# Unused one-pass matmuls at stage borders of the second block of a two-block layer kernel

## The chip, the cores and the metric

The kernel runs on one core of a Trainium2 chip. The metric is the device time of one execution in microseconds (us); the median of three runs is given. TensorE is called PE here, VectorE DVE, ScalarE ACT, GpSimd POOL, and SyncE, which issues most transfers, SP.

## What is computed

Two transformer-like blocks run one after the other on 512 tokens of width 1024. The first one is a convolution branch and a windowed attention, followed by a layer of 16384 experts of which each token picks 16 in each of 8 heads. The second one, where nearly all of the change lies, is cut to its shape here:

```python
def second_block(x, mem, positions, norm_g, ..., w_out):
    h = rms_norm(x, norm_g[l])
    p = h @ w_in[l]
    (p_r, p_k, p_v, p_w, p_a, z_a, p_q, p_sk, p_sv, z_b,
     p_xq, z_c, p_gate) = jnp.split(p, split_points, axis=-1)
    y_a = rwkv7_mix(p_r, p_k, p_v, p_w, p_a, ...) * silu(z_a)
    y_b = sliding_window_sink_attn(p_q, p_sk, p_sv, positions, ...) * silu(z_b)
    y_c = memory_cross_attn(p_xq, mem, ...) * silu(z_c)
    gates = sigmoid(p_gate).reshape(bsz, t, 3, D_MODEL)
    merged = (gates[:, :, 0] * (y_a @ w_proj_a[l]) + gates[:, :, 1] * (y_b @ w_proj_b[l])
              + gates[:, :, 2] * (y_c @ w_proj_c[l]))
    return x + merged @ w_out[l]
```

## The kernel before

The program is a row of stages. Each stage is a block in which every engine has its own hand-written order of instructions, and at the end of a block all five engines wait for one another. No instruction of the next block starts on any engine before the slowest one has arrived; in the order of PE this shows as a branch that waits for the release of a barrier. Below, a border is such a place, and the release is the moment at which all engines go on.

Large products run in units of 24 matmuls. A unit is one 128 wide column block of weights, 8 pieces deep. Both operands are held as a high and a low part in a rounded 32-bit format (fp32r), and `product` (lines 152 to 156) makes three one-pass matmuls of 128 x 512 of each piece: high by high, low by high, high by low. The weights of a unit come through a ring. SP loads them (L197), ACT makes the high part (L205) and POOL the low part (L222). `hT` is the normalised input, transposed, as high and low part, and it stays in place for the whole block.

The second block has 46 units that no stage needs at once: gates and projections used later. They are the work of the class `Filler`. Each stage calls `fill.pe(pe, steps)`, and a step is one piece, so three matmuls. Their results go through banks 6 and 7, are copied by ACT (L293) and stored to DRAM by SP (L302). What is left at the end is done by `catch_up`, which waits for the stores. The stages of the second block that the change touches, in order:

- `project_tiles` (rwz): 13 units with `hT`, whose weights are there when the stage begins.
- `rwkv_prepare`: four fp32 matmuls L2001 that wait for a tanh of ACT, filler steps, four more (L2007), filler steps.
- `rwkv_solve`, which runs four times, t from 0 to 3: 16 small fp32 matmuls of 64 rows (L2171, 32 records in the profile), then filler steps.
- `fetch`, run three times (rwgate, swz, xqz): SP brings a part of the stored results back, ACT applies Silu (L1786), PE does 3, 14 or 8 filler steps.
- `rotate`: DVE turns queries and keys (L1901 to L1903) while PE does 18 filler steps.
- `attention` (attn2) follows it: for each of 32 pairs of a token block and a head, scores (L497), softmax on DVE and ACT, a transposing product (L507), the values (L519), and one filler step.
- `rms_over_partitions` (xqnorm): ACT squares four tiles, PE sums them (L1672), DVE and ACT make the root, PE does two filler steps, spreads the root (L1681) and does eight more.
- `catch_up`: the last filler unit.
- `merge_second`: 12 units with the three branches' outputs. PE waits for DVE's high and low parts (L2608, L2610), and DVE multiplies by gates and adds (L2620, L2626).
- `out_residual` (wout2): 8 units into eight banks, then DVE adds x (L1029) and SP stores the output.

Of the kernel before, what the change touches and what calls it, by code (L numbers as in the profile page):

```python
# [27 lines left out]
P = 128  # L28
# [208 lines left out]
        return Split(self.high[:, u % 2], self.low[:, u % RING])  # L237


class Filler:  # L240


# [66 lines left out]
            sp.wait_ge(self.stored[i], 16 * ((self.sent + 1 - i) // 2))  # L309


def catch_up(nc, fill):

    with nc.Block() as block:
        @block.tensor
        def _(pe):
            fill.pe(pe, DT * FILL2)

        @block.scalar
        def _(act):  # L320
            fill.act(act, fill.done)

        @block.sync
        def _(sp):
            fill.sp(sp)
            fill.wait_stored(sp)

        @block.gpsimd
        def _(pool):
            fill.w.low_parts(pool)  # L330
# [341 lines left out]
def first_block(nc, w, bank, cols, const, rows, subkeys, given, x, hT, mem_store, dump):  # L672

    ident, ones = const.whole("ident"), const.whole("ones")
    with ExitStack() as outer:
        attnT = split_tensor(nc, outer, "attnT", [P, DT, T])

        z_store = nc.dram_tensor("z1_store", (FILL1, P, T), F32, kind="Internal").ap()
        with ExitStack() as inner:
            conv = split_tensor(nc, inner, "convT", [P, DT, T])  # L680
            convT = conv.whole
            qkvT = inner.enter_context(nc.sbuf_tensor("qkvT", [P, 12, T], F32))
            norm_to_T(nc, w, bank, "norm1", x, TT, cols.whole("norm1"), ident, hT, first_unit("z1") + RING)
# [14 lines left out]
            units = []  # L698
            for b in range(TT):
                lo, hi = max(b - 1, 0), min(b + 2, TT)  # L700
                for i in range(8):
                    for e in range(2):
                        h = HEADS1[i][e]
                        a, part = i // 4, slice(e * HD, (e + 1) * HD)
                        kv = 2 * a + e
                        units.append(dict(
                            q=qkvT[part, i, b * P:(b + 1) * P], k=qkvT[part, 8 + a, lo * P:hi * P],
                            bias=(const.whole("dist")[:, (lo - b + 1) * P:(hi - b + 1) * P], -SLOPES[h] * HD ** 0.5),
                            v=[v_tok[:, c, kv * HD:(kv + 1) * HD] for c in range(lo, hi)],
                            sink=cols("sink", h), sink_scaled=sink8[:, h:h + 1], half=e))  # L710
            at = lambda g: (slice(None), slice(4 * (g % 2), 4 * (g % 2) + 4), slice((g // 2) * P, (g // 2 + 1) * P))
            attention(nc, bank, "attn1", units, scale=HD ** -0.5, sink=True, ident=ident,
                      out=lambda g: attnT.high[at(g)], out_low=lambda g: attnT.low[at(g)], group=8, dim=HD, fill=fill,
                      fill_steps=2)
            catch_up(nc, fill)
            assert fill.done == FILL1
        with ExitStack() as inner:
            mergedT = split_tensor(nc, inner, "mergedT", [P, DT, T])
            merge_first(nc, w, bank, z_store, attnT, mergedT)
            out_residual(nc, w, bank, "wout1", mergedT, x, first_unit("query") + RING, 0.5)  # L720
    dump("x1", x)
    with ExitStack() as inner:
        h2 = inner.enter_context(nc.sbuf_tensor("h2", [P, TT, D], F32))
        score_store = nc.dram_tensor("score_store", (TT, PH, P, 2, NKEYS), F32, kind="Internal").ap()
        norm_to_T(nc, w, bank, "norm2", x, TT, None, ident, hT, first_unit("query") + RING, scaled=h2,
                  row_gain=rows[:])
        experts(nc, w, bank, cols, const, ident, subkeys, score_store, h2, hT, given["peer_uv"], x, rows[:],
                given["rows1"][:, D:2 * D], given["mem"], mem_store)
    dump("y", x)
# [250 lines left out]
                    split_merged(nc, dve, mergedT, f, high_ready)  # L980


def out_residual(nc, w, bank, name, mergedT, x, prefetch, scale, store=None):


    with Stage(nc, name) as st:
        ready, added, stored = st.sem("ready"), st.sem("added"), st.sem("stored")
        u0 = first_unit(name)
        with st.block() as block:
# [8 lines left out]

            @block.tensor
            def _(pe):  # L1000
                for k in range(DT):
                    ring = w.wait(pe, u0 + k)
                    for t in range(TT):
                        for e in range(2):
                            mm = product(nc, bank[2 * t + e][:], mergedT[:, k, t * P:(t + 1) * P],
                                         ring[:, 4 * e:4 * e + 4], k == 0, k == DT - 1)
                            if k == DT - 1 and (t, e) != (TT - 1, 1):
                                mm.then_inc(ready, 1)
                    mm.then_inc(w.done, 1)
# [614 lines left out]
def project_tiles(nc, w, bank, name, unit, count, src, takers, prefetch, loads=()):  # L1624
# [3 lines left out]
    with Stage(nc, name) as st:  # L1628
        kept, loaded = st.sem("kept"), st.sem("loaded")
        u0 = first_unit(unit)  # L1630
        with st.block() as block:
# [9 lines left out]
            def _(pe):  # L1641
                def four_tiles(i, first, count=RING):
                    for j in range(count):
                        ring = w.wait(pe, u0 + j, i)
                        if not first:

                            pe.wait_ge(kept, i * RING + (j - RING + 1))
                        for k in range(DT):
                            mm = product(nc, bank[j][:, 0:width], ring[:, k], src[:, k], k == 0, k == DT - 1)
                        mm.then_inc(w.done, 1)  # L1650
                rounds(pe, count // RING, four_tiles)
                if count % RING:
                    four_tiles(count // RING, False, count % RING)
# [32 lines left out]
def rms_over_partitions(nc, bank, name, tiles, gains, selector, ident, fill, steps):  # L1686
# [5 lines left out]
    with Stage(nc, name) as st:  # L1692
# [4 lines left out]
        with st.block() as block:  # L1697
            @block.tensor
            def _(pe):
                for i in range(len(tiles)):  # L1700
                    pe.wait_ge(squared, i + 1)
                    mm = group_sums(nc, bank[0][:, i * columns:(i + 1) * columns], sq[:, i], selector)
# [39 lines left out]
def second_block(nc, ctx, w, bank, a, x, hT, mem_store, out, dump, load):  # L1742
# [18 lines left out]
    y_low = [same_place(nc, f"y{n}T_low", y_shape, o) for n, o in zip("abc", offsets)]  # L1761
    sliding_branch(nc, w, bank, a, cols, const, yT[1], dump, load, fill)
    memory_branch(nc, bank, cols, const, mem_store, yT[2], dump, fill)
    catch_up(nc, fill)
    with ExitStack() as s:
        mergedT = split_tensor(nc, s, "merged2T", [P, DT, T])
        merge_second(nc, w, bank, yT, y_low, z_store, mergedT)
        out_residual(nc, w, bank, "wout2", mergedT, x, sum(n for _, n in UNITS), 1.0, store=out)


def fetch(nc, name, fill, first, z, silu, steps, more=()):

    n = z.shape[1]
    with Stage(nc, name) as st, st.block() as block:
        arrived, done = st.sem("arrived"), st.sem("done")

        @block.tensor
        def _(pe):
            fill.pe(pe, steps)

        @block.scalar
# [21 lines left out]
def memory_branch(nc, bank, cols, const, mem_store, y, dump, fill):  # L1803

    ident, ones = const.whole("ident"), const.whole("ones")
    with ExitStack() as s:
        kv = s.enter_context(nc.sbuf_tensor("mem_kv", [P, 2, 1024], F32))
        kT, v_tok = (kv[:, e].rearrange("p (a b) -> p a b", a=n) for e, n in ((0, 4), (1, 2)))
        qz = s.enter_context(nc.sbuf_tensor("xqz", [P, 8, T], F32))
        fetch(nc, "xqz", fill, 14, qz[:], 4, 8, [(kv[:], mem_store)])  # L1810
        rms_over_partitions(nc, bank, "xqnorm", [qz[:, n] for n in range(4)], 4 * [cols.whole("xq_g")], ones[:, 0:1],
                            ident, fill, (2, 8))
        units = [dict(q=qz[:, h, b * P:(b + 1) * P], k=kT[:, h], bias=None,
# [14 lines left out]
def sliding_branch(nc, w, bank, a, cols, const, y, dump, load, fill):  # L1828

    ident = const.whole("ident")  # L1830
    with ExitStack() as s:
# [1 line left out]
        z = s.enter_context(nc.sbuf_tensor("swz", [P, 10, T], F32))  # L1833
        v_tok = s.enter_context(nc.sbuf_tensor("vs_tok", [P, TT, P], F32))
        sink8 = s.enter_context(nc.sbuf_tensor("sink8_2", [P, 8], F32))
        fetch(nc, "swz", fill, 4, z[:], 6, 14)
        rms_over_partitions(nc, bank, "sqknorm", [z[:, n] for n in range(5)], 4 * [cols.whole("q_g")] + [cols.whole("k_g")],
                            const.whole("halves")[:, 0:P:HD], ident, fill, (3, 10))
        turn_tiles(nc, w, bank, "turn_vs", [([z[:, 5, t * P:(t + 1) * P]], v_tok[:, t]) for t in range(TT)], ident, 0)
# [21 lines left out]
def rotate(nc, bank, a, cols, const, z, load, fill):  # L1861
# [7 lines left out]
    with Stage(nc, "rope") as st:  # L1869
# [8 lines left out]
        with st.block() as block:  # L1878
# [27 lines left out]
            def _(pe):  # L1906
                for i in range(5):
                    nc.tensor.matmul(bank[i][:], const.whole("swap"), z[:, i], start=True, stop=True).then_inc(swapped, 1)
                fill.pe(pe, 18)

            @block.scalar
            def _(act):
# [15 lines left out]
def rwkv_branch(nc, w, bank, a, cols, const, hT, y, dump, load, fill, tables):  # L1928
# [7 lines left out]
    with ExitStack() as s:  # L1936
# [24 lines left out]
            rwkv_output(nc, bank, const, t, R, B, Kt, toks, ZW, WT, S, y, fill)  # L1961

        gate = toks["A"]
        fetch(nc, "rwgate", fill, 0, gate[:], 0, 3)
        rwkv_finish(nc, bank, cols, halves, ident, y, bonus, gate, toks["B"], dump, fill)


def rwkv_prepare(nc, bank, a, cols, const, z, R, A, B, Kt, bonus, r_end, toks, load, fill):
    halves = const.whole("halves")
    with Stage(nc, "rwprep") as st:  # L1970
# [6 lines left out]
        with st.block() as block:  # L1977
# [18 lines left out]

            @block.tensor
            def _(pe):
                pe.wait_ge(tanh_ready, 1)
                for t in range(TT):  # L2000
                    nc.tensor.matmul(bank[t][:], tl[0:CH, t * P:(t + 1) * P], lora[0:CH, :], start=True,  # L2001
# [150 lines left out]
def rwkv_solve(nc, bank, const, t, A, B, Kt, toks, ZW, WT, y, fill):  # L2152
# [4 lines left out]
    with Stage(nc, f"solve{t}") as st:  # L2157
# [6 lines left out]
        with st.block() as block:  # L2164
            @block.tensor
            def _(pe):

                for e, left in enumerate((B, Kt)):
                    for h in range(8):
                        part, c, cols = head(h)  # L2170
# [371 lines left out]
    dump("ya", y)  # L2542


def merge_second(nc, w, bank, yT, y_low, z_store, mergedT):


    u0, g0 = first_unit("merge"), FILL2 - 24
# [5 lines left out]
    with Stage(nc, "merge2") as st:  # L2554
# [7 lines left out]
        with st.block() as block:  # L2562
# [11 lines left out]
            @block.tensor  # L2574
            def _(pe):

                for n in range(12):
                    ring = w.wait(pe, u0 + n)
                    if n >= 2:
# [207 lines left out]
```

## Time and profile before

| | us |
|---|---|
| median of three runs | 2996.11 |
| lowest and highest run | 2995.95, 2999.30 |
| profiled execution, its own time | 2995.75 |
| span of the trace, first to last instruction | 2993.9 |
| PE busy | 2505.0 (84%) |
| DVE busy | 1741.2 (58%) |
| mean granted PE clock | 0.954 |

The profile lists the work of each engine by kernel line, with what released an engine from a wait. "PEq" as releaser is PE's own sequencer: at a stage's first matmul that is the border. The granted clock of PE is 1.00 at 2.4 GHz and 0.50 at 1.2 GHz. The busy length of one matmul record has the pipeline's depth in it, so the pace of a row of matmuls is read as a stretch of time divided by the matmuls in it. The second block runs from 2032 us to the end.

### The profile page before, as it was taken

The numbers are of one execution on the slowest core, as the hardware profiler recorded it, in microseconds if no ns is written. First come the engines' busy times: TensorE is split into PE (matmuls) and PEld (weight loads), VectorE is DVE, ScalarE is ACT, GpSimd is POOL, SyncE is SP. The second block draws the span as 40 slices with busy tenths as digits, with TensorE's granted clock in tenths as the row PEclk, the third lists the DMA queues.
The fourth block names the chain that finished last, engine by engine and source line by source line (L and its number), as shares of the span: only waits on it lengthen the run. The fifth ranks groups of instructions, "written<-read, shape, count | busy, mean of one in ns | idle before, by whom it ended". The sixth has DMA issues, their size and how long they took to land. (4 is left out here: it accounts for less than half of the span.)

```text
span 2993.9 us, 30870 instructions
## 1 busy us (share of the span) xinstructions
PE 2505.0 (84%) x10382; PEld 1601.2 (53%) x10382; DVE 1741.2 (58%) x3956; ACT 892.5 (30%) x1997; POOL 848.8 (28%) x649
## 2 busy tenths in 40 slices
PE   6997999978987788777777777778889999789888
PEld 4885666765543343222222232227678887555766
DVE  5998556536776777667766676650353332255353
ACT  3223434133333243223322232222322220234331
POOL 0001110435544455334333343323221110111133
PEclk9998999989999998999999999999899999879899
DMA  3332111429999999999999999972121110221242
GB/s 119 109 104 76 61 46 50 137 96 404 422 421 420 421 419 418 421 421 416 417 413 416 413 411 422 406 328 92 63 65 53 43 54 23 92 67 42 85 156 91
DMA packets 132922, 683.46 MB, mean 228 GB/s; under 512 B 13472, under 2 KB 24992, under 8 KB 66976
## 3 DMA queue, kind: packets, MB, share of 16 engines
q0 software_dynamic: 73728, 536.90, 43.3%
q1 hardware_dynamic: 59040, 144.61, 14.5%
q8 instruction: 83, 1.36, 0.2%
q14 instruction: 71, 0.58, 0.1%
HBM read 655.77 MB, written 25.69 MB: 228 GB/s over the span
## 5 line engine op out<-in xcount | busy, mean ns | idle before, releaser
L1611 PE MATMUL bank<-peer_uv,peer_diag 128*128 128x512 f32 x2048 | 965.7, 616 | 295.0 <-ACT peer_diag L1284 294.7
L1511 DVE SCALAR_TENSOR_TENSOR peer_uv<-peer_uv,h 128x1024 f32<-128x1024 f32 x512 | 642.2, 1265 | 383.0 <-DMA peer_uv<-in_peer_uv,peer_index 382.9
L1611 PEld LDWEIGHTS bank<-peer_uv,peer_diag 128*128 128x128 f32 x2048 | 382.8, 195 | 838.0 <-issue 833.5
L1319 POOL DMA_INDIRECT peer_uv<-in_peer_uv,peer_index x512 | 529.8, 1035 | 747.4 <-PE bank L1611 662.2
L222 POOL TENSOR_TENSOR weight_low<-weight_ring,weight_high 128x1024 fp32r<-128x1024 f32 x107 | 260.5, 2435 | 1308.4 <-ACT weight_high L205 1308.4
L154 PE MATMUL bank<-hT_high,weight_high 128*128 128x512 f32 x952 | 416.6, 438 | 34.3 <-POOL weight_low L222 13.4
L155 PE MATMUL bank<-hT_low,weight_high 128*128 128x512 f32 x952 | 382.6, 402 | 0.0
L156 PE MATMUL bank<-hT_high,weight_low 128*128 128x512 f32 x952 | 381.9, 401 | 0.0
L205 ACT ACTIVATE weight_high<-weight_ring 128x1024 fp32r<-128x1024 f32 x171 | 180.6, 1056 | 578.5 <-PE bank L156 490.6
L1279 ACT ACTIVATE peer_gelu<-peer_dots 128x2 f32<-128x2 f32 x256 | 52.0, 203 | 789.4 <-DVE peer_uv L1511 789.3
L154 PEld LDWEIGHTS bank<-hT_high,weight_high 128*128 128x128 f32 x952 | 186.0, 195 | 93.3 <-issue 38.3
L1284 ACT ACTIVATE peer_diag<-const,peer_weight 128x128 f32<-128x128 f32 x512 | 177.5, 393 | 118.7 <-DVE peer_weight L1423 117.8
L155 PEld LDWEIGHTS bank<-hT_low,weight_high 128*128 128x128 f32 x952 | 186.3, 196 | 41.4 <-issue 9.6
L156 PEld LDWEIGHTS bank<-hT_high,weight_low 128*128 128x128 f32 x952 | 185.6, 195 | 41.6
L548 DVE SCALAR_TENSOR_TENSOR attn_logit<-const,bank 128x256 f32<-128x256 f32 (+2 forms) x96 | 43.5, 453 | 122.2 <-PE bank L497 122.2
L507 PE MATMUL bank<-attn_diag,attn_prob 128*128 128x128 f32 x496 | 83.7, 295 | 9.1 <-issue 5.4
L507 PEld LDWEIGHTS bank<-attn_diag,attn_prob 128*128 128x128 f32 x496 | 65.3, 191 | 48.2 <-issue 36.5
L827 DVE SCALAR_TENSOR_TENSOR convT_whole<-z_u,cols,convT_whole 128x512 f32<-128x512 f32 x120 | 89.5, 746 | 0.0
L827 DVE SCALAR_TENSOR_TENSOR z_odd<-z_u,cols,z_odd 128x512 f32<-128x512 f32 x112 | 83.6, 746 | 0.0
L1423 DVE SCALAR_TENSOR_TENSOR peer_weight<-peer_gelu,peer_r,peer_e 128x2 f32<-128x2 f32 x256 | 59.0, 230 | 38.9 <-ACT peer_gelu L1279 38.9
L611 ACT ACTIVATE attn_sinkexp<-cols,attn_negtop 128x1 f32<-128x1 f32 x96 | 28.3, 294 | 156.5 <-DVE attn_negtop L557 156.4
L230 POOL TENSOR_TENSOR weight_low<-weight_ring,weight_high 128x1024 fp32r<-128x1024 f32 x24 | 58.0, 2415 | 46.8 <-ACT weight_high L205 46.5
(393 smaller groups left out, 3243.7 us busy)
## 6 DMA issues: line engine op xcount, KB each, us to landing
weight_ring<-in_weights SPq DMA_DIRECT2D x171, 512.0 KB, 3.6
z_store<-fill_stage SPq DMA_DIRECT2D x70, 256.0 KB, 2.7
peer_uv<-in_peer_uv,peer_index POOLq DMA_INDIRECT x512, 14.1
merge_z<-z_store SPq DMA_DIRECT2D x8, 768.0 KB, 4.9
merge_z<-z_store SPq DMA_DIRECT2D x12, 512.0 KB, 4.6
score_store<-peer_work SPq DMA_DIRECT2D x16, 256.0 KB, 13.9
peer_sc<-score_store SPq DMA_DIRECT2D x24, 128.0 KB, 8.7
swz<-z_store SPq DMA_DIRECT2D x1, 2560.0 KB, 9.9
```

The source lines that it names most:

```text
L154: nc.tensor.matmul(to, left[0], right[0], start=start, stop=False)
L155: nc.tensor.matmul(to, left[0], right[1], start=False, stop=False)
L156: return nc.tensor.matmul(to, left[1], right[0], start=False, stop=stop)
L205: self.nc.scalar.activation(self.high[:, u % 2].bitcast(F32R), self.ring[:, u % RING], ACT.Copy).then_inc(self.high_ready, 1)
L222: self.nc.gpsimd.tensor_tensor(self.low[:, slot].bitcast(F32R), self.ring[:, slot], self.high[:, u % 2], ALU.subtract).then_inc(self.split, 1)
L507: mm = nc.tensor.matmul(bank[2 + i % 2][:, c * P:(c + 1) * P], prob[:, i % B, c * P:(c + 1) * P], diag[:, i % B], start=True, stop=True)
L827: nc.vector.scalar_tensor_tensor(to, u[:, c, k:k + T], cols("conv_w", k * DT + c), to, ALU.mult, ALU.add).then_inc(tap_done, 1)
L1284: nc.scalar.activation(diag[:, p % SLOTS], ident, ACT.Copy, scale=weight[:, p % TOPK:p % TOPK + 1]).then_inc(diag_ready, 1)
L1319: pool.indirect_dma_start(uv[:, p % SLOTS], None, peer_uv, bass.IndirectOffsetOnAxis(index[:, n % 2, p % TOPK:p % TOPK + 1], 0)).then_inc( ...
L1423: nc.vector.scalar_tensor_tensor(weight[:, at], gelu[:, at], r[:, b:b + 1], e[:, b, at], ALU.mult, ALU.mult).then_inc(weight_ready, 1)
L1511: nc.vector.scalar_tensor_tensor(uv[:, p % SLOTS, 0:D], uv[:, p % SLOTS, 0:D], 1.0, h2[:, t], ALU.mult, ALU.mult, accum_out=dots[:, p % TO ...
L1611: mm = nc.tensor.matmul(bank[2 * (t % 2) + c][:], diag[:, p % SLOTS], uv[:, p % SLOTS, D + c * 512:D + (c + 1) * 512], start=(p % PICKS == ...
```

## The change

A new helper issues n one-pass matmuls of 128 x 512, with the first high piece of `hT` as both operands, into a bank whose content nobody reads. The order of PE's instructions has ten new groups with 206 matmuls in all: 12 at rwz, 22 at `rwkv_prepare`, 12 at the first `rwkv_solve`, 18 at rwgate, 26 at the end of `rotate`, 18 at xqz, 22 at xqnorm, 12 at `catch_up`, 34 at `merge_second` and 30 at wout2. `catch_up` also runs in the first block, where its condition leaves the group out. Nothing else moves, and no wait is added or taken away.

```diff
+def keep_running(nc, bank, hT, n):
+    high = hT.high[:, 0].bitcast(F32R)
+    for _ in range(n):
+        nc.tensor.matmul(bank[:], high[:, 0:P], high, start=True, stop=True)
...
 def catch_up(nc, bank, fill):
...
+            if fill.step < DT * fill.limit:
+                keep_running(nc, bank[0], fill.items[0][0], 12)
             fill.pe(pe, DT * FILL2)
...
 def out_residual(nc, w, bank, name, mergedT, x, prefetch, scale, hT, store=None):
...
+                if name == "wout2":
+                    keep_running(nc, bank[0], hT, 30)
                 for k in range(DT):
...
 def project_tiles(...):
...
+                keep_running(nc, bank[0], src, 12)
                 rounds(pe, count // RING, four_tiles)
...
 def rms_over_partitions(...):
...
+                if len(tiles) == 4:
+                    keep_running(nc, bank[5], fill.items[0][0], 22)
                 for i in range(len(tiles)):
                     pe.wait_ge(squared, i + 1)
...
 def fetch(nc, name, bank, fill, first, z, silu, steps, more=()):
...
+            if steps < 10:
+                keep_running(nc, bank, fill.items[0][0], 18)
             fill.pe(pe, steps)
...
 def rotate(...):
...
                 fill.pe(pe, 18)
+                keep_running(nc, bank[5], fill.items[0][0], 26)
...
 def rwkv_prepare(...):
...
+                keep_running(nc, bank[0], fill.items[0][0], 22)
                 pe.wait_ge(tanh_ready, 1)
...
 def rwkv_solve(...):
...
+                keep_running(nc, bank[0], fill.items[0][0], 12 if t == 0 else 0)
                 for e, left in enumerate((B, Kt)):
...
 def merge_second(nc, w, bank, yT, y_low, z_store, mergedT, hT):
...
+                keep_running(nc, bank[0], hT, 34)
                 for n in range(12):
```

Two places show where the groups stand against the borders. The first is PE at the entry of the last stage, wout2, as it was: the last matmuls of `merge_second`, the border, and the first product.

```order
L155 MATMUL bank<-ycT_low,weight_high 128x512
L156 MATMUL bank<-merge_y_high,weight_low 128x512
L2562 UNCONDITIONAL_BRANCH
L999 UNCONDITIONAL_BRANCH [waits barrier_Pool_Activation_PE_DVE_SP_release]
L154 MATMUL bank<-weight_high,merged2T_high 128x512 [waits weights_split]
```

The same place with the change:

```order
L156 MATMUL bank<-merge_y_high,weight_low 128x512
L2580 UNCONDITIONAL_BRANCH
L1008 UNCONDITIONAL_BRANCH [waits barrier_Pool_Activation_PE_DVE_SP_release]
L244 MATMUL bank<-hT_high 128x512 x30
L154 MATMUL bank<-weight_high,merged2T_high 128x512 [waits weights_split]
L155 MATMUL bank<-weight_low,merged2T_high 128x512
```

The 30 new matmuls stand behind the wait for the border's release and ahead of the first product. Nine of the ten groups stand like this, behind the release. The tenth is the one at the end of `rotate`. PE there before the change, with the last filler step, the border, and the first score of attn2:

```order
L154 MATMUL bank<-hT_high,weight_high 128x512
L155 MATMUL bank<-hT_low,weight_high 128x512
L156 MATMUL bank<-hT_high,weight_low 128x512
L1878 UNCONDITIONAL_BRANCH
L488 UNCONDITIONAL_BRANCH [waits barrier_Pool_Activation_PE_DVE_SP_release]
L497 MATMUL bank<-swz 128x128
```

And with the change:

```order
L155 MATMUL bank<-hT_low,weight_high 128x512
L156 MATMUL bank<-hT_high,weight_low 128x512
L244 MATMUL bank<-hT_high 128x512 x26
L1894 UNCONDITIONAL_BRANCH
L497 UNCONDITIONAL_BRANCH [waits barrier_Pool_Activation_PE_DVE_SP_release]
L506 MATMUL bank<-swz 128x128
```

Here the group stands ahead of the border, behind the stage's own work.

## Rows read from the trace of the kernel before

**Rows 1.** The page: busy time of each engine.
```profile
PE 2505.0 (84%) x10382; PEld 1601.2 (53%) x10382; DVE 1741.2 (58%) x3956; ACT 892.5 (30%) x1997; POOL 848.8 (28%) x649
```

**Rows 2.** PE's waits, second block: line, what released it, us, times, longest.
```profile
PE bank L154 <- DVE yaT_low L2610: 8.6, 1, 8.6
...
PE bank L154 <- PEq L1822: 8.1, 2, 5.0
PE bank L154 <- PEq L2562: 7.5, 1, 7.5
...
PE bank L497 <- PEq L1841: 6.5, 1, 6.5
PE bank L2001 <- ACT rw_V_tok L2015: 6.2, 1, 6.2
PE bank L1672 <- ACT xqnorm_sq L1714: 6.0, 1, 6.0
...
PE bank L2492 <- PEq L1774: 5.9, 1, 5.9
...
PE bank L2171 <- PEq L646: 3.7, 1, 3.7
PE bank L154 <- PEq L1146: 3.7, 1, 3.7
```

**Rows 3.** Busy time, count of each engine, and PE's granted clock, in chosen stretches.
```profile
core 0: us, PE busy (x) PEld busy (x) DVE busy (x) ACT busy (x) POOL busy (x), PEclk, DMA share, GB/s
2032.18:2036.59 4.41, 4.41 (x10) 3.45 (x11) 0.00 (x0) 0.00 (x0) 0.00 (x0) 0.50 0.69 229
2111.44:2122.00 10.56, 10.56 (x16) 5.24 (x17) 8.87 (x14) 3.74 (x5) 0.00 (x0) 0.50 0.00 0
2219.18:2227.76 8.58, 8.58 (x40) 7.61 (x41) 5.22 (x6) 0.00 (x0) 0.00 (x0) 0.50 0.00 0
2282.82:2287.37 4.55, 4.55 (x40) 4.13 (x41) 3.25 (x5) 0.00 (x0) 0.00 (x0) 1.00 0.00 0
2569.60:2572.80 3.20, 3.19 (x4) 1.42 (x5) 1.08 (x2) 0.00 (x0) 0.00 (x0) 0.55 0.00 0
2672.35:2685.27 12.92, 12.30 (x30) 7.47 (x30) 6.33 (x24) 6.49 (x20) 2.35 (x1) 0.51 0.32 93
2786.25:2793.10 6.85, 6.85 (x32) 6.85 (x33) 0.00 (x0) 2.79 (x4) 0.00 (x0) 0.50 0.22 80
2807.46:2808.59 1.13, 1.13 (x6) 0.94 (x5) 0.58 (x3) 0.61 (x3) 0.00 (x0) 1.00 0.78 286
2848.70:2856.00 7.30, 7.30 (x24) 5.53 (x24) 0.00 (x0) 1.43 (x2) 2.37 (x1) 0.77 0.33 108
2864.62:2869.45 4.83, 4.83 (x11) 3.77 (x12) 4.76 (x4) 2.03 (x2) 0.00 (x0) 0.50 0.39 142
2942.24:2948.10 5.86, 5.86 (x14) 4.60 (x15) 0.00 (x0) 0.00 (x0) 0.00 (x0) 0.51 0.00 0
2948.10:2989.90 41.80, 41.77 (x180) 33.21 (x178) 4.83 (x7) 6.35 (x6) 14.36 (x6) 1.00 0.22 75
```

**Rows 4.** Instructions in order of time: start, length, engine, line, and the idle time before.
```profile
2109.06 1.28 ACT L2015 ACT_TABLE_LOAD   x1 [2.25 <-PEq L1631]
...
2567.11 2.19 ACT L1786 ACTIVATE rw_A_tok<-rw_A_tok 128x512 f32<-128x512 f32 x4 [2.95 <-DMA rw_A_tok<-z_store]
...
2665.47 0.39 PE L156 MATMUL bank<-hT_high,weight_low 128*128 128x512 f32 x1
...
2670.87 0.69 DVE L1903 TENSOR_TENSOR swz<-rope_straight,rope_crossed 128x512 f32<-128x512 f32 x1
...
2785.57 2.19 ACT L1714 ACTIVATE xqnorm_sq<-xqz 128x512 f32<-128x512 f32 x4 [0.29 <-PEq L1774]
...
2857.63 0.32 SPq L302 DMA_DIRECT2D z_store<-fill_stage  x1
2860.88 1.40 SPq L2569 DMA_DIRECT2D merge_z<-z_store  x3
```

More of the change, by code:

```diff
@@ L309, in wait_stored, with catch_up @@
             sp.wait_ge(self.stored[i], 16 * ((self.sent + 1 - i) // 2))
-def catch_up(nc, fill):
+def catch_up(nc, bank, fill):
     with nc.Block() as block:
@@ L714, in first_block @@
                       fill_steps=2)
-            catch_up(nc, fill)
+            catch_up(nc, bank, fill)
             assert fill.done == FILL1
@@ L719, in first_block @@
             merge_first(nc, w, bank, z_store, attnT, mergedT)
-            out_residual(nc, w, bank, "wout1", mergedT, x, first_unit("query") + RING, 0.5)
+            out_residual(nc, w, bank, "wout1", mergedT, x, first_unit("query") + RING, 0.5, hT)
     dump("x1", x)
@@ L980, in _, with out_residual @@
                     split_merged(nc, dve, mergedT, f, high_ready)
-def out_residual(nc, w, bank, name, mergedT, x, prefetch, scale, store=None):
+def out_residual(nc, w, bank, name, mergedT, x, prefetch, scale, hT, store=None):
     with Stage(nc, name) as st:
@@ L1763, in second_block, with fetch @@
     memory_branch(nc, bank, cols, const, mem_store, yT[2], dump, fill)
-    catch_up(nc, fill)
+    catch_up(nc, bank, fill)
     with ExitStack() as s:
         mergedT = split_tensor(nc, s, "merged2T", [P, DT, T])
-        merge_second(nc, w, bank, yT, y_low, z_store, mergedT)
-        out_residual(nc, w, bank, "wout2", mergedT, x, sum(n for _, n in UNITS), 1.0, store=out)
-def fetch(nc, name, fill, first, z, silu, steps, more=()):
+        merge_second(nc, w, bank, yT, y_low, z_store, mergedT, hT)
+        out_residual(nc, w, bank, "wout2", mergedT, x, sum(n for _, n in UNITS), 1.0, hT, store=out)
+def fetch(nc, name, bank, fill, first, z, silu, steps, more=()):
     n = z.shape[1]
@@ L1809, in memory_branch @@
         qz = s.enter_context(nc.sbuf_tensor("xqz", [P, 8, T], F32))
-        fetch(nc, "xqz", fill, 14, qz[:], 4, 8, [(kv[:], mem_store)])
+        fetch(nc, "xqz", bank[0], fill, 14, qz[:], 4, 8, [(kv[:], mem_store)])
         rms_over_partitions(nc, bank, "xqnorm", [qz[:, n] for n in range(4)], 4 * [cols.whole("xq_g")], ones[:, 0:1],
@@ L1835, in sliding_branch @@
         sink8 = s.enter_context(nc.sbuf_tensor("sink8_2", [P, 8], F32))
-        fetch(nc, "swz", fill, 4, z[:], 6, 14)
+        fetch(nc, "swz", bank[0], fill, 4, z[:], 6, 14)
         rms_over_partitions(nc, bank, "sqknorm", [z[:, n] for n in range(5)], 4 * [cols.whole("q_g")] + [cols.whole("k_g")],
@@ L1963, in rwkv_branch @@
         gate = toks["A"]
-        fetch(nc, "rwgate", fill, 0, gate[:], 0, 3)
+        fetch(nc, "rwgate", bank[0], fill, 0, gate[:], 0, 3)
         rwkv_finish(nc, bank, cols, halves, ident, y, bonus, gate, toks["B"], dump, fill)
@@ L2542, in rwkv_finish, with merge_second @@
     dump("ya", y)
-def merge_second(nc, w, bank, yT, y_low, z_store, mergedT):
+def merge_second(nc, w, bank, yT, y_low, z_store, mergedT, hT):
     u0, g0 = first_unit("merge"), FILL2 - 24
```

## The prediction

> **What bounds the kernel now.** I read the page first, then the list of PE's waits, then the stretches around each border of the second block with their granted clock, and last the single instructions there. The page says that PE is busy for 84% of 2993.9 us [rows 1]. The change lies in the second block alone, the last 960 us, so the question is who ends each stage there. The waits of PE in that part are few and nearly all of them lie at borders [rows 2]: 7.5 us ahead of wout2, 8.6 ahead of merge, 6.5 ahead of attn2, 3.7 ahead of rwz and of the first solve. Within the stages PE works through its list almost without a gap (41.77 busy of 41.80 us in wout2, [rows 3]), so the time of most stages is the length of PE's list. What is added to that list behind a release adds time, unless PE would have stood there anyway.
>
> After most borders PE's clock is 0.50. The first 10 matmuls of rwz take 4.41 us, 0.43 us each; 180 in wout2 at clock 1.00 take 41.80 us, 0.23 each [rows 3]. So a one-pass matmul of 128 x 512 costs 0.43 us at 1.2 GHz and 0.23 at 2.4 GHz, and each us that PE works at the half clock could be 0.53 us (0.23/0.43). How long does PE work at half clock from the first dense matmul until the clock rises? 4.4 us in rwz, 4.8 in merge, 5.9 in wout2 [rows 3]. I take 5.0 as a mean. An unused group pays this climb itself and hands a full clock to what follows.
>
> The Trainium skill has the gap between matmuls in the page "TensorE: Matmul & The Clock Gate", section "Back-to-back issue gap": 512 columns at 1.2 GHz, so 427 ns, and 512 at 2.4 GHz plus 2.5 ns, so 216. The trace agrees on the first, and on the second it shows 0.23. By the page's figure the sum below would be about 1 us smaller, an estimate from that page; the trace's own duration is used.
>
> **The important reading is where a wait lies: ahead of the release or behind it.** The 7.5 us ahead of wout2 have PEq as the releaser, that is, PE stood at the border while DVE ended merge [rows 2]. Behind the release the first product starts at once. In the new order the 30 matmuls stand behind the same release. They can't use these 7.5 us; they begin where the product began. Only in three stages does PE also wait behind the release: in rwprep for tanh (release at 2109.0 by ACT's first row [rows 4], first matmul at 2111.4 [rows 3], so 2.4 us), in merge for DVE's parts (release 2860.9 [rows 4], first matmul 2864.6 [rows 3], 3.7 us) and in xqnorm (ACT starts at 2785.6 [rows 4], PE at 2786.3, 0.7 us).
>
> **The change part by part.** Positive means later.
>
> 1. rwz, 12 matmuls. PE starts at the release now and has work to the end. The climb of 4.4 us happens either way, so the 12 cost their full-clock price: 12 x 0.23 = +2.8.
>
> 2. rwprep, 22. At 0.43 for 5.0 us (11.6 of them), then 10.4 x 0.23 = 2.4: 7.4 us from 2109.0, so to 2116.4, 5.0 after the old start. The stretch from 2111.44 to 2122.00, all at half clock [rows 3], shrinks from 10.56 to 10.56 x 0.53 = 5.6, saving 4.9. Sum +0.1.
>
> 3. first solve, 12. All at half clock: 12 x 0.43 = 5.1. Behind them 40 records took 8.58 us at 0.50; the same records in the second solve took 4.55 at 1.00 [rows 3], saving 4.0. Sum +1.1. If the clock has not risen by the end of the 12, the sparse 64-row matmuls that follow may leave it low, as they did before (it rose only after 8.6 us), and the stage loses up to 5.1.
>
> 4. rwgate, 18. PE comes in at full clock, so 4.1 us. The stage ends with ACT's Silus at 2569.3 [rows 4], and PE had been idle for 5.9 us at the next border [rows 2], so they are covered. The next stage would start at 1.00 instead of half clock for 3.2 us [rows 3]; DVE works tile by tile behind PE there, so I count the first half of the possible 1.7: -0.9. If the clock falls anyway, 0.
>
> 5. rotate, 26, ahead of the border. PE's last filler matmul starts at 2665.47, its successor's slot is 2665.7, and 26 x 0.23 = 6.0 brings PE to 2671.7; DVE ends the stage at 2670.87 + 0.69 = 2671.56 [rows 4]. So +0.2 at the border, and attn2 starts at full clock. Its first 12.92 us were at half clock with 30 records [rows 3]. They are five score steps, two of them with the transposing product. A score step at full clock in attn3 took 1.13 us [rows 3] (a slightly cheaper one); I take 1.2, and 1.7 for the two: 3 x 1.2 + 2 x 1.7 = 7.0. The first softmax chain is then likely to be late by some 1.2 us. That leaves 12.92 - 8.2 = 4.7. With the border, -4.5. DVE was busy for only 6.3 of the 12.9 us [rows 3], so it is not the next bound. Bounds: 0 if the clock falls before attn2, -5.7 if nothing stalls.
>
> 6. xqz, 18: at half clock for 5.0, then 6.4 x 0.23 = 1.5, so 6.5 us. The filler's 24 matmuls behind it gain some 2.4, since their first 12 ran at half clock. PE ends 4.1 later. It had been idle for 6.0 us before the first sum of xqnorm [rows 2], 5.3 of them ahead of the release, while ACT worked. Covered: 0. The gain shows only in the next term.
>
> 7. xqnorm, 22, now at full clock: 22 x 0.23 = 5.1 from 2785.6, to 2790.7, 4.4 after the old start. The 32 sums took 6.85 us at half clock [rows 3], 3.7 at full: they end at 2794.3 instead of 2793.1, +1.2. I leave it at +1.2, since the clock may fall after these tiny sums. If it stays up, the sum is -1.1; if PE is slow again on the spreads, +2.5.
>
> 8. catch_up, 12. PE's last matmul leads to ACT's copy, to the store at 2857.63 and to its landing, which releases merge at 2860.88 [rows 4]. PE is on this path from its first matmul. Its 24 matmuls take 7.30 us, partly at half clock (0.77 on the mean, [rows 3]). The fall and rise of the clock come at the same time with 12 more ahead, so +2.8.
>
> 9. merge, 34. 5.0 us at half clock (11.6), 22.4 x 0.23 = 5.2: 10.2 from 2860.9, so 2871.1 instead of 2864.6, +6.5. The first 11 products, 4.83 us at half clock [rows 3], would take 2.5, -2.3. Sum +4.2. Behind that PE is never stopped to the end of the stage, so all of it reaches the border.
>
> 10. wout2, 30. 5.0 + 18.4 x 0.23 = 9.2 later; the first 14 products go from 5.86 us [rows 3] to 3.2, -2.6. Sum +6.6. DVE's additions and the output store hang on PE's last unit.
>
> Sum: 2.8 + 0.1 + 1.1 - 0.9 - 4.5 + 0 + 1.2 + 2.8 + 4.2 + 6.6 = +13.4 us. The profiled execution took 2995.75 us, 1.9 outside the span; with +13.4 it is 3009.2. It lies 0.4 under the median of 2996.11, so the median comes to 3009.5.
>
> **The rivals.** *A: the groups run in the waits and cost nothing.* This is the faster one. Its mechanism is that PE would work ahead of the release, so that 7.5 us before wout2 or 3.7 before the solve are filled. The gains alone, by the steps above: rwz 10 x 0.2 = 2.1, rwprep 4.9, solve 4.0, rwgate 0.9, attn2 4.7, xqnorm 6.85 - 3.7 = 3.2 and some 2.3 behind it, catch_up 8 x 0.2 = 1.6, merge 2.3, wout2 2.6, in all 28.6, so 2967.5 us. It decides as soon as the unused matmuls start before the stage's other engines do. Against it: the first matmul of wout2 waited on PEq, with the weights ready, and the new group stands behind the same release. For it only that the gains are real. The Trainium skill's advice in "TensorE: Matmul & The Clock Gate", section "Why this matters for your kernels", to leave no idle gaps between bursts of matmuls, would give this result if followed in the gap itself. The trace's rows show that the gap is at the border, where this code can't reach.
>
> *B: the two doubtful gains fail.* The clock is low in the solve in spite of the group (+5.1 instead of +1.1) and attn2 starts low (+0.2 instead of -4.5): 13.4 + 4.0 + 4.7 = 22.1, so 3018.2. For it: the solve's group ends just when the clock is due.
>
> *C: the climbs are short and the sums keep their clock.* With a climb of 3.6 us instead of 5.0 each of terms 2, 3, 9 and 10 loses 1.4 x 0.47 = 0.7, and xqnorm ends at -1.1: 13.4 - 2.6 - 2.3 = 8.5. If the catch-up's 2.8 were hidden as well by a store that is late for another reason, 5.7, so 3001.8, within what counts as no change.
>
> **How the numbers follow.** About 0.2%, 6 us, is what a measurement of this kernel can tell from no change. The forecast, between +6 and +20, has 0.73; B 0.10; C down to no change 0.11; A, with less than its full gain too, 0.06. The range is to reach from C's lower end, 3001.5, to some way towards B, 3016.5. What is left out is B's upper part and A, together under 0.2. Faster 0.06, same 0.11, slower 0.83. The terms that carry the forecast, 1, 8, 9 and 10, make +16.4 and rest on little but counts and the pace of a matmul.
>
> **What would show it.** In the new profile the unused matmuls' line should have 206 records. In wout2 it should start within 0.1 us of the release and its first product about 9 us later, at clock 1.00; merge's first product should come some 10 us behind the release; attn2's first 5 score steps should take 8 us rather than 12.9 at clock 1.00; the fetches should not be longer. The prediction is wrong if the groups start before the release, if products in wout2 or merge were held by something else than PE, or if the clock rises much earlier than 5 us after a border.

## The result: 1.2% slower, and the profile after

| | before | changed |
|---|---|---|
| median, us | 2997.63 (4 runs) | 3033.41 (4 runs) |
| lowest and highest run, us | 2995.95, 2999.30 | 3030.63, 3040.75 |
| profiled execution, us | 2995.75 | 3034.99 |
| span of its trace, us | 2993.9 | 3033.1 |

The ratio is 1.0123, with a 95% interval of 1.0103 to 1.0143. The direction was the forecast one. The size was not: the median moved by 35.8 us where 13.4 was forecast, and it lies 17 us above the range.

The page of the changed kernel answers to [rows 1]: 206 records more on PE, and 63 us more of its time.

```profile
span 3033.1 us, 31282 instructions
...
PE 2568.0 (85%) x10588; PEld 1646.8 (54%) x10588; DVE 1738.6 (57%) x3956; ACT 892.1 (29%) x1997; POOL 851.0 (28%) x649
```

The instructions at the release of wout2, in the changed kernel (start, length, engine, line, idle time before):

```profile
2974.80 1.19 PE L244 MATMUL bank<-hT_high 128*128 128x512 f32 x2 [7.54 <-PEq L2580]
...
2984.13 0.39 PE L154 MATMUL bank<-weight_high,merged2T_high 128*128 128x512 f32 x1
```

PE still stands for 7.54 us ahead of the release, as in [rows 2]. Then it runs the 30 unused matmuls for 9.3 us, and only then the first product. This is what the prediction said of the group.

The stretches of the changed kernel that answer to [rows 3] are rwz, solve, attn2 in three parts, catch_up, merge and wout2. Each row has the stretch and its length, busy time and count of PE, PEld, DVE, ACT and POOL, PE's granted clock, the share of the DMA engines and GB/s:

```profile
2036.37:2116.22 79.85, 75.99 (x324) 62.36 (x324) 0.00 (x0) 20.10 (x26) 31.06 (x13) 0.97 0.32 105
2227.36:2244.49 17.13, 16.64 (x92) 13.39 (x92) 5.21 (x6) 3.84 (x7) 2.36 (x1) 0.85 0.14 47
2685.06:2693.20 8.14, 6.44 (x27) 4.16 (x28) 6.29 (x23) 5.46 (x16) 2.36 (x1) 1.00 0.44 145
2693.20:2731.00 37.80, 37.80 (x92) 21.15 (x90) 14.23 (x57) 12.34 (x45) 4.71 (x2) 0.50 0.09 32
2731.00:2793.14 62.14, 58.26 (x282) 37.05 (x281) 30.69 (x117) 24.53 (x81) 7.07 (x3) 1.00 0.12 38
2874.32:2888.88 14.56, 9.92 (x36) 7.75 (x36) 0.00 (x0) 3.08 (x4) 4.72 (x2) 0.85 0.31 108
2888.88:2974.74 85.86, 78.32 (x322) 62.10 (x322) 59.84 (x62) 26.41 (x25) 30.39 (x12) 0.94 0.45 147
2974.74:3032.84 58.10, 54.28 (x222) 43.32 (x222) 5.53 (x8) 6.37 (x6) 14.41 (x6) 0.94 0.21 73
```

The same stages of the kernel before, where the three rows of attn2 are one:

```profile
2219.12:2234.51 15.39, 15.09 (x80) 13.07 (x80) 5.22 (x6) 3.83 (x7) 2.36 (x1) 0.72 0.16 51
2672.30:2769.46 97.16, 91.54 (x399) 56.84 (x399) 51.76 (x196) 42.36 (x141) 14.18 (x6) 0.93 0.15 49
2785.54:2806.20 20.66, 19.71 (x94) 17.81 (x94) 3.42 (x6) 5.12 (x8) 2.35 (x1) 0.70 0.11 39
2848.49:2860.87 12.38, 7.33 (x24) 5.57 (x24) 0.00 (x0) 3.09 (x4) 4.71 (x2) 0.79 0.39 127
2860.87:2942.18 81.31, 70.08 (x288) 55.40 (x288) 59.80 (x62) 26.40 (x25) 30.36 (x12) 0.92 0.47 155
2942.18:2993.64 51.46, 47.63 (x192) 37.84 (x192) 5.53 (x8) 6.35 (x6) 14.36 (x6) 0.93 0.23 82
```

Most stages come near what was forecast; the table below has them. wout2 goes from 51.46 to 58.10 us, merge from 81.31 to 85.86. The exception is attn2. It begins at clock 1.00, as wanted. After 8.14 us the clock falls, and then PE works for 37.80 us without a gap at 0.50, 92 matmuls in all. The stage takes 108.1 us instead of 97.2. The forecast had 92.5.

What happened just ahead of the fall, in the changed kernel:

```profile
2689.52 2.36 POOL L222 TENSOR_TENSOR weight_low<-weight_ring,weight_high 128x1024 fp32r<-128x1024 f32 x1 [14.14 <-ACT weight_high L205]
...
2689.75 2.15 DVE L578 TENSOR_TENSOR attn_full<-attn_total,attn_sinkexp 128x1 f32<-128x1 f32 x1
...
2692.26 0.28 DVE L587 TENSOR_SCALAR attn_diag<-const,attn_recip 128x128 f32<-128x128 f32 x1
...
2692.68 0.35 PE L516 MATMUL bank<-attn_diag,attn_prob 128*128 128x128 f32 x1 [1.64 <-DVE attn_diag L587]
```

DVE's addition of one column, 0.15 us elsewhere, lasts 2.15 us, until POOL's subtraction of 2.36 us has ended. DVE's diagonal comes late, and PE stands for 1.64 us in the fifth score step. The clock falls half a microsecond after PE goes on. The second profile of the changed kernel has the same lengths at the same place: 2.36 us of POOL, 2.15 of DVE, and PE standing for 1.65.

### The profile page after: what moved, and what is told of

The parts are those of the page before. It is cut to its first block and busy times, and to the rows that moved or that the text cites. A ratio compares the mean times of both kernels' runs of the same rounds, so it can differ in the third digit from the quotient of the medians.

```text
span 3033.1 us, 31282 instructions
## 1 busy us (share of the span) xinstructions
PE 2568.0 (85%) x10588; PEld 1646.8 (54%) x10588; DVE 1738.6 (57%) x3956; ACT 892.1 (29%) x1997; POOL 851.0 (28%) x649
## 5 line engine op out<-in xcount | busy, mean ns | idle before, releaser
L222 POOL TENSOR_TENSOR weight_low<-weight_ring,weight_high 128x1024 fp32r<-128x1024 f32 x107 | 260.4, 2434 | 1348.0 <-ACT weight_high L205 1348.0
L244 PE MATMUL bank<-hT_high 128*128 128x512 f32 x206 | 65.0, 483 | 34.0 <-PEq L1838 7.9
L620 ACT ACTIVATE attn_sinkexp<-cols,attn_negtop 128x1 f32<-128x1 f32 x96 | 28.2, 294 | 171.2 <-DVE attn_negtop L566 170.9
```

The source lines that it names most:

```text
L222: self.nc.gpsimd.tensor_tensor(self.low[:, slot].bitcast(F32R), self.ring[:, slot], self.high[:, u % 2], ALU.subtract).then_inc(self.split, 1)
L244: nc.tensor.matmul(bank[:], high[:, 0:P], high, start=True, stop=True)
```

## The experiments

Two theories of the missing 22 us. **A:** the group at the end of `rotate` costs attn2 11 us by itself: the stage starts fast, meets its first softmax stall, the clock falls in it, and the thin steps that follow leave it low. **B:** attn2's long stretch at half clock came from the shift by the other nine groups, or by chance.

The kernel before was run again beside each set of experiments, on three chips. Of those runs 12 of 31, 4 of 30 and 3 of 17 took over 3008 us, so a difference of 10 us between two medians is hard to tell, and the profiles of the stages carry most of what follows.

**One group alone, at rotate.** All other counts are zero.

```diff
                 fill.pe(pe, 18)
+                keep_running(nc, bank[5], fill.items[0][0], 26)
```

> The kernel before with one group alone: the 26 unused matmuls at the end of rotate. Theory A (this group costs attn2 11 us: the stage then starts at full clock, meets the first softmax stall early, the clock falls there, and the sparse steps leave it low): attn2 about 108 us instead of 97.2, the whole +8 to +13 us over before. Theory B (the other nine groups shifted attn2 into a bad phase of the clock, or it was chance): attn2 92 to 98 us, the whole -5 to +1 us.

Measured: ten runs between 3012.8 and 3022.0 us, median 3014.4, with the kernel before beside it at a median of 3003.2. With the scatter of the latter (2995.9 to 3032.5) the ratio does not tell them apart (1.0012, 0.9981 to 1.0044). attn2 and the part of it at half clock:

```profile
2676.62:2786.27 109.65, 104.02 (x399) 63.20 (x399) 51.41 (x196) 42.34 (x141) 14.15 (x6) 0.81 0.13 44
2685.90:2726.80 40.90, 40.90 (x100) 23.05 (x100) 15.37 (x61) 12.39 (x45) 4.71 (x2) 0.50 0.08 26
```

attn2 is 12.5 us longer than in the first profile of before, with this group as the only change. PE stood for 1.66 us at the same place before the clock fell. Theory A holds on this point.

**All groups but that one.**

> The changed kernel without the group of 26 at the end of rotate; the other nine stay. Theory A: attn2 back at 97 us, the whole 11 us under the changed kernel, so +22 to +28 us over before. Theory B: attn2 at 104 us or more in spite of it, the whole +33 to +40 us.

Measured: median 3024.4 us, ten runs from 3019.8 to 3041.9, ratio 1.0065 (1.0032 to 1.0097). Against the median beside it, 3003.2, that is +21.2, just under what theory A said, and four of the ten runs are over 3030. The profile is that of the slowest run, and its attn2 is not at the 97 us of theory A. It is long as well, in a stage that starts at half clock:

```profile
2684.86:2801.27 116.41, 111.83 (x399) 67.92 (x399) 50.83 (x196) 42.70 (x141) 14.16 (x6) 0.74 0.13 41
```

Here the clock did not fall in the stage. It stood at 0.50 from the entry on for 59.6 us, with the same first steps, and the same wait of 0.62 us in the fourth of them, behind which it rose after 12.9 us in the kernel before. So both theories have a part: a long stretch at half clock comes without the group too, by chance as far as the runs show. The run with 30 matmuls at the end of merge, told below, has an attn2 of 120.83 us although everything ahead of it is the kernel before. Its clock rose early, 4.6 us into the stage; then PE stood for 1.89 us, again for DVE's diagonal beside POOL's subtraction, and the clock fell in this wait.

**The group at rotate, with a guard in attn2.** Six unused matmuls behind each of the steps 3, 4 and 5.

```diff
                     fill.pe(pe, fill_steps)
+                    if name == "attn2" and i in (3, 4, 5):
+                        keep_running(nc, bank[4 + (i // group + 1) % 2], fill.items[0][0], 6)
                     fill.mark()
```

> The 26 at the end of rotate as the only group, and in attn2 six unused matmuls behind each of steps 3, 4 and 5, where PE stood still for 0.8 and 1.6 us in the changed kernel. Theory A with its mechanism (the stall drops the clock, nothing else): the clock stays at 1.00 in attn2, the stage takes 92 to 95 us with the 18 matmuls' 4.2 us in it, the whole -5 to -1 us. Theory A without that mechanism: attn2 again over 104 us. Theory B: no less than the run with the group alone plus 4 us.

Measured: median 2999.1 us, ratio to before 0.9961 (0.9929 to 0.9992), no run over 3007. attn2 is at clock 1.00 throughout:

```profile
2672.40:2767.32 94.92, 90.38 (x417) 57.08 (x417) 51.78 (x196) 42.22 (x141) 14.20 (x6) 1.00 0.15 51
```

With 18 more matmuls in it the stage is 14.7 us shorter than without them. (The 0.8 us in the expectation is PE's wait at the stage's entry, 0.77 us, and no wait between steps.) The wait in the fifth step is still there, but the guard has filled most of it:

```profile
2680.07 0.46 PE L516 MATMUL bank<-attn_diag,attn_prob 128*128 128x128 f32 x2 [0.32 <-DVE attn_diag L589]
```

This bears out theory A. The guard does two things at once: it shortens the wait and it adds full-width matmuls around it. Which of the two holds the clock is not separated by it.

**The guard too late,** behind steps 9, 10 and 11. There the same line of code picks bank 4, where the first eight heads' output is being summed, so that output is overwritten; the work and its time are the same.

> As the run with the rotate group and the guard, but the three times six unused matmuls stand behind steps 9, 10 and 11 of attn2, after the clock has fallen. If the sparse steps hold the clock down and dense work raises it: half clock from step 4 to about step 10 or 11, attn2 100 to 105 us. If the low stretch ends by itself after some 40 us whatever PE does: attn2 109.7 + 4 us or more.

Measured: attn2 105.17 us, at the upper end of the forecast for dense work that raises the clock, and far from the rival's 113.7; median of the runs 3009.1. The clock rose at the end of the first of the three groups:

```profile
2688.00:2708.40 20.40, 20.40 (x49) 12.05 (x49) 7.94 (x30) 5.65 (x23) 2.36 (x1) 0.50 0.04 14
...
2706.14 2.61 PE L244 MATMUL bank<-hT_high 128*128 128x512 f32 x6
```

The low stretch ends at 2708.4, within that group, and is 20.4 us long rather than 40.9. Attention's steps keep PE busy for all of 20.40 us here, 40.90 above and 37.80 in the changed kernel, and the clock stays at 0.50. With no such group the low stretches ended too, but later: after about 31 us in the second profile of the changed kernel, then 37.8, 40.9, 59.6 and 61.4. That the group ended this one is likely and rests on one profile.

**The guard alone,** with no group at rotate.

> The kernel before with the six unused matmuls behind each of steps 3, 4 and 5 of attn2, and no group at rotate. Reading C (what lengthens attn2 is a fall of the clock in its first steps, and the kernel before has it by chance too, as the profiles with attn2 at 116 and 121 us show): attn2 95 to 99 us in all runs, the slow tail of the kernel before (runs over 3008 us) gone. Reading D (the guard only helps a stage that starts at full clock): attn2 still over 105 us in some runs, runs over 3015 us remain.

Measured: ten runs between 3001.9 and 3011.9 us, median 3007.0, ratio 1.0012 (0.9992 to 1.0033). attn2 is 100.57 us, outside reading C's 95 to 99, and three of the ten runs are over 3008, so that tail is not gone. No run is over 3012, but of the kernel before beside it only 2 of 30 were, so ten runs can't show that the guard removed them. Neither reading is borne out. The clock rose after 13.0 us, much as in the first profile of before, and the stage is 3.4 us longer than there: alone the guard costs nearly its 18 matmuls. The gain was seen only with the group at rotate ahead of it.

**30 unused matmuls ahead of the release of wout2,** not behind it. They stand at the end of `merge_second`, and no other group runs.

```diff
                     mm.then_inc(w.done, 1)
+                keep_running(nc, bank[4], hT, 30)
```

> The kernel before with 30 unused matmuls at the end of merge, so ahead of the border where PE stood for 7.5 us, instead of behind it. The prediction's rule (what stands ahead of the release is free, what stands behind it costs its full price): wout2 starts at clock 1.00 and takes 48.9 instead of 51.5 us, merge stays at 81.3, the whole -2.6 us. The rival (PE's end of merge sets the border, or the clock falls at the border anyway): 0 to +7 us.

Measured, attn2, wout2 and merge:

```profile
2673.32:2794.15 120.83, 114.98 (x399) 69.71 (x399) 51.08 (x196) 42.79 (x141) 14.12 (x6) 0.73 0.12 39
2965.93:3014.78 48.85, 45.03 (x192) 35.91 (x192) 5.53 (x8) 6.35 (x6) 14.35 (x6) 1.00 0.24 86
2884.64:2965.93 81.29, 76.81 (x318) 61.02 (x318) 59.89 (x62) 26.42 (x25) 30.41 (x12) 0.95 0.45 156
```

wout2 takes 48.85 us at clock 1.00, 2.6 less than before, and merge is not longer. Behind the release the same 30 cost 6.6 us. The whole shows nothing of this (0.998, 0.994 to 1.002), since attn2 scatters by more. The stage decides here, not the sum. In attn2 the wait in which the clock fell was this one:

```profile
2681.64 0.77 PE L516 MATMUL bank<-attn_diag,attn_prob 128*128 128x128 f32 x2 [1.89 <-DVE attn_diag L587]
```

**The changed kernel with the guard.**

> The changed kernel with the guard in attn2's steps 3, 4 and 5 (18 matmuls more). If the prediction failed in the term of attn2 alone: attn2 95 us instead of 108, the other nine groups unchanged (rwz +2.9, solve +1.7, catch_up +2.2, merge +4.5, wout2 +6.7), the whole 3016 to 3021 us. If other stages had taken part: over 3025 us.

Measured: median 3020.6 us, ratio 1.0055 (1.0033 to 1.0076), within the forecast; the kernel before beside it had a median of 3002.6, so the medians lie 18.1 apart. attn2:

```profile
2679.20:2774.05 94.85, 90.33 (x417) 57.08 (x417) 51.82 (x196) 42.25 (x141) 14.21 (x6) 1.00 0.15 50
```

The forecast's sum with this attn2, -2.3 us (97.16 to 94.85) in place of -4.7, is 15.8 us.

**Both kernels once more.**

> The changed kernel once more. If attn2's long stretch at half clock belongs to the change: attn2 104 to 116 us, ten runs between 3024 and 3042 us. If it was chance in one profile: attn2 92 to 98 us, several runs under 3020 us.

Measured: attn2 105.09 us at a mean clock of 0.85, in a run of 3024.0; the four runs reach from 3024.0 to 3030.5. The long stretch belongs to the change.

> The kernel before once more, to see where its own spread lies. Its profile should differ from the first one only in the stages whose clock differs: attn1 206.2 or 209.9 us, attn2 97 or over 105 us, the others within 2 us. If its spread lay in the transfers of the expert stage instead, that stage (1398.5 us) would differ by over 5 us.

Measured: 2995.7 to 3031.0 us in ten runs. The profiled one, 3003.7 us, has attn1 at 209.8 instead of 206.2 us, a stage of the convolution at 44.6 instead of 43.3, and the expert stage 1.3 longer. Its attn2 is 97.74. The forecast that the others agree within 2 us missed: the stage behind rwprep took some 3.3 us more, and the first stage of the mixing's output 3.1 less (14.8 instead of 17.9, at clock 1.00 instead of 0.81). The two slowest runs, 3018.4 and 3031.0 us, have no profile.

**All groups where PE stands still.** Groups of 14, 12, 26, 10, 10, 20 and 30 ahead of a release (the end of rwz, of the turning stage before the solve, of rotate, in both gating multiplies, at the end of catch_up and of merge), behind a release only what fits a wait there (9, 18, 18 and 15), and the guard.

```diff
-                keep_running(nc, bank[0], fill.items[0][0], 22)
+                keep_running(nc, bank[0], fill.items[0][0], 9)
                 pe.wait_ge(tanh_ready, 1)
...
             fill.pe(pe, DT * FILL2)
+            if last:
+                keep_running(nc, bank[0], fill.items[0][0], 20)
...
-                keep_running(nc, bank[0], hT, 34)
+                keep_running(nc, bank[0], hT, 15)
```

> Unused matmuls only where PE stands still: ahead of the release (14 at the end of rwz, 12 at the end of the turning stage before the first solve, 26 at the end of rotate, 10 in each gating multiply, 20 at the end of catch_up, 30 at the end of merge), and behind it only as many as fit a wait there (9 rwprep, 18 rwgate, 18 xqz, 15 merge); in attn2 six behind each of steps 3, 4, 5. If a group costs only what it adds behind a release: rwprep -4.9 us, solve -3.9, rwfinish -0.9, attn2 -2.3, xqnorm up to -3.2, catch_up -1.6, merge -2.3, wout2 -2.6, in all about -20 us against before, 2976 to 2984 us. Rival (the clock falls at each border whatever stands ahead of it): -5 us or less.

Measured: median 2984.9 us, nine runs between 2982.5 and 2988.3, ratio 0.9932 (0.9910 to 0.9954). It is faster than both kernels, and steadier, and 0.9 us above the forecast range. Its stages rwprep, solve, attn2, xqnorm, catch_up, merge and wout2:

```profile
2117.64:2145.26 27.62, 27.28 (x100) 18.21 (x100) 25.53 (x31) 11.46 (x15) 5.16 (x2) 1.00 0.18 58
2224.32:2236.20 11.88, 11.39 (x80) 9.59 (x80) 5.21 (x6) 3.84 (x7) 2.36 (x1) 1.00 0.19 68
2671.15:2766.07 94.92, 90.38 (x417) 57.08 (x417) 51.80 (x196) 42.22 (x141) 14.19 (x6) 1.00 0.16 50
2783.67:2804.51 20.84, 19.89 (x94) 17.99 (x94) 3.42 (x6) 5.12 (x8) 2.35 (x1) 0.70 0.12 39
2847.05:2857.89 10.84, 10.25 (x44) 8.18 (x44) 0.00 (x0) 3.08 (x4) 4.79 (x2) 1.00 0.46 145
2857.89:2937.10 79.21, 78.42 (x333) 62.16 (x333) 59.80 (x62) 26.42 (x25) 30.43 (x12) 1.00 0.49 160
2937.10:2985.94 48.84, 45.03 (x192) 35.91 (x192) 5.53 (x8) 6.35 (x6) 14.35 (x6) 1.00 0.25 87
```

Six of the seven are at 1.00 and near what was expected: -5.0, -3.5, -2.2, -1.5, -2.1 and -2.6 us. xqnorm gained nothing. Its clock was 0.70 again: xqz's matmuls ran at 1.00, ended sooner, and PE then stood for 4.3 us. The gating multiply behind attn2 lost: its group took 3.9 us where DVE needed 2.3, so that stage took 4.1 us instead of 2.6. The profiled run itself, 2988.06 us, is only 7.7 us under the first one of before. Its second block is 16 us shorter, its first block and experts 8.4 longer, the first attention with 210.4 instead of 206.2 among them.

**Real work as the guard.** Two more filler steps in each of attn2's steps 3 to 5 instead of the 18 unused matmuls.

> The version with the groups ahead of the releases, but in attn2's steps 3, 4 and 5 two more steps of the filler's real work each, instead of six unused matmuls; catch_up has six steps less to do. If dense work of any kind holds the clock there: attn2 95 us, clock 1.00, and catch_up 4 us shorter than with the unused ones (10.8), the whole 2979 to 2984 us. If the real steps cannot hold it, since they wait for weights: attn2 over 100 us.

Measured: median 2985.3 us (0.9925 to 0.9960), 1.3 above the forecast. attn2 took 96.24 us at clock 1.00, so real work holds the clock as well, and catch_up fell from 10.8 to 6.5 us. PE stood once for 1.32 us in the first steps, waiting for weights, and once for 1.40 us near the end, and the clock did not fall:

```profile
2686.82 0.50 PE L154 MATMUL bank<-hT_high,weight_high 128*128 128x512 f32 x1 [1.32 <-POOL weight_low L222]
```

xqz rose to 16.91 us:

```profile
2779.01:2795.92 16.91, 9.80 (x42) 7.80 (x42) 0.00 (x0) 4.90 (x7) 2.34 (x1) 0.94 0.64 233
...
ACT xqz L1809 <- DMA mem_kv<-mem_store: 9.8, 1, 9.8
...
2793.11 0.57 ACT L300 ACTIVATE fill_stage<-bank 128x512 f32<-128x512 f32 x1
2793.71 0.32 SPq L309 DMA_DIRECT2D z_store<-fill_stage  x1
```

ACT waited 9.8 us there for the fetch to land, but it waited 9.7 in the kernel before as well, where the stage took 13.5 us. New is what stands behind the Silus. The filler's order has moved by six steps, so a unit ends in this stage: ACT copies its result, SP stores it at 2793.71, and the next stage begins only at 2795.9. Whether another number of steps avoids that was not tried. On the sum the two versions can't be told apart.

## Why the prediction was wrong, point by point

The stages of two profiles of the changed kernel and of the one with the guard, less those of the first profile of before, us:

| term | forecast | first | second | with guard |
|---|---|---|---|---|
| 1 rwz | +2.8 | +2.9 | +2.9 | +2.7 |
| 2 rwprep | +0.1 | -0.6 | -0.6 | -0.6 |
| 3 solve | +1.1 | +1.7 | +1.7 | +1.6 |
| 4 rwgate and the stage behind | -0.9 | -0.7 | +0.1 | 0.0 |
| 5 rotate and attn2 | -4.5 | +11.1 | +8.1 | -2.1 |
| 6, 7 xqz and xqnorm | +1.2 | +2.1 | +2.1 | +2.0 |
| 8 catch_up | +2.8 | +2.2 | +2.6 | +2.6 |
| 9 merge | +4.2 | +4.6 | +3.2 | +3.3 |
| 10 wout2 | +6.6 | +6.6 | +6.0 | +6.0 |
| other stages of the second block | 0 | +5.0 | +2.8 | +3.0 |
| first block, experts | 0 | +4.2 | -0.6 | +0.1 |
| sum | +13.4 | +39.2 | +28.2 | +18.3 |

**The reading of where a wait lies was right.** Terms 1, 8, 9 and 10 were to carry the forecast with +16.4, and they measured 16.3, 14.7 and 14.6. The 30 matmuls moved ahead of the release confirmed it from the other side.

**Term 5 failed, by 15.6 us in the first profile and 12.6 in the second.** The step was "3 x 1.2 + 2 x 1.7 = 7.0. The first softmax chain is then likely to be late by some 1.2 us." The wait was seen, at about its right size (1.2 us forecast, 1.64 measured), and priced as a wait alone. That the clock would fall behind it, and stay at 0.50 through 37.80 us of attention's steps, was in no bound: the text gave "0 if the clock falls before attn2, -5.7 if nothing stalls". In five profiles the clock was at 1.00 when PE stood for 1.64 to 1.89 us in attn2's first steps (both of the changed kernel, the group at rotate alone, the late guard, the 30 matmuls at merge), and it fell each time. Where that wait was cut to 0.3 us by the guard it stayed. In both profiles of before the clock is at 0.50 there, the wait is 0.62 us, and the clock rises after about 13 us; the run without the rotate group had the same wait and no rise for 59.6 us, so the 97 us of before are partly luck. A term with gains only was a term whose other end had not been looked for. A hint was there, in the solve's row of [rows 3]: 8.58 us of unbroken work at 0.50.

**Term 7 failed in its premise, by a small amount.** It had PE enter xqnorm at full clock, "22 x 0.23 = 5.1". PE had stood ahead of the release, the clock was 0.50 for the first 2.7 us, and the group took 6.6 us:

```profile
2809.41 6.78 PE L244 MATMUL bank<-hT_high 128*128 128x512 f32 x22 [2.32 <-PEq L1788]
```

The 32 sums behind it took 3.5 us, near the 3.7 forecast. The two terms 6 and 7 came to +2.1 instead of +1.2. rwprep and the solve lie within 0.7 us.

**What was left out.** Stages that the change doesn't touch took 3 to 5 us more in the second block, where their clock fell once more or once less than before. The first block, ahead of every group, moved by +4.2 us in one profile and -0.6 in the other; its first attention takes 206.2 or 209.8 us in kernels alike. Its clock is 1.00 in the first case and 0.97 in the second. Nothing in the runs gives a cause for these, and the range had no room for them. In the two profiles the sums, +39.2 and +28.2, are made of 18 to 19 us of the nine other terms (17.9 forecast), 11.1 or 8.1 of term 5, and 9.2 or 2.2 of stages that the change leaves alone; the median's +35.8 lies between. The right direction was no luck, since the nine terms alone carry it. The rivals did no better: B, the nearest, had attn2 at +0.2, and its other half, a solve at low clock behind the group, did not happen.

## What to carry to other kernels

Work that only keeps an engine awake has to stand ahead of the barrier at which the engine waits; behind it the same instructions are paid in full unless the engine waits there too, and the profile tells the two apart by the releaser. Ahead of the barrier, too, they are free only for as long as the engine would have stood: the group of 10 in the gating multiply cost 1.5 us. Before a stage is given a faster start, look for the first wait that it then meets, and look in the trace for whether the work behind it has ever won the clock back. And where the median scatters by 1%, judge each group by its own stage.

## What the runs showed of the hardware

PE can be busy for 61.16 of 61.40 us and stay at 1.2 GHz. In the run with the 30 matmuls at the end of merge:

```profile
2681.40:2742.80 61.40, 61.16 (x153) 35.77 (x153) 21.17 (x92) 17.85 (x64) 4.72 (x3) 0.50 0.07 26
```

The same mix of matmuls also ran at 2.4 GHz for 62 us in the changed kernel, and for the whole stage with the guard. So the stage was seen at two speeds, each for 60 us and more. From the high one it went to the low one in five profiles, each time in or within 2 us behind a wait of 1.64 to 1.89 us; waits of 0.8 to 1.40 us in this stage were not followed by a fall. What brings it back from the low one is open but for the one profile with the late guard. The kernel before runs from 2995.5 to 3032.5 us; its profiled runs, and those of its copies up to attn2, give attn2 values of 97.2, 97.7 and 120.8 us.

A DVE addition of one column took 2.15 us instead of 0.15 while POOL subtracted a tile of 1024 columns. In the run with the 30 matmuls at merge it was the diagonal, 2.25 us instead of 0.28, that ended 0.1 us behind POOL's subtraction of 2.34. That it is POOL that holds DVE is read from the rows' common end and was not tried by an experiment of its own.
